# Centring the layer norm on GpSimd ahead of the experts, and no gathered rows in three units before the last stage

## The reference, cut to what matters

```python
def layer_norm(x, g, b):
    mu = jnp.mean(xf, axis=-1, keepdims=True)
    var = jnp.mean(jnp.square(xf - mu), axis=-1, keepdims=True)
    y = (xf - mu) * lax.rsqrt(var + LN_EPS)
    return y * g + b
...
h = layer_norm(ALPHA * h + mix, ln1_g, ln1_b)
ffn = peer_ffn(h, peer_wq, peer_subkeys, peer_u, peer_v)
h = layer_norm(ALPHA * h + ffn, ln2_g, ln2_b)
...
# peer_ffn, for a token: qh = x @ wq; best 16 experts of each head by two sets of sub-keys
act = gelu(einsum('td,thkd->thk', xc, u[expert]))
out = einsum('thk,thkd->td', gate * act, v[expert])
```

## Time and profile before

| | |
|---|---|
| median of 3 runs | 2832.28 us (2826.26 to 2835.13) |
| profiled execution: time | 2836.36 us |
| profiled execution: span from first to last instruction | 2834.5 us |
| mean granted TensorE clock | 0.987 of full speed |
| PE, DVE, ACT, POOL busy | 96%, 68%, 49%, 14% of the span |
| DMA over the span | 236 GB/s |

### The profile page before, as it was taken

One profiled execution on the slowest core, in us unless ns is written; L12 is line 12 of the kernel. 1 busy time (PEld: TensorE's weight loads), 2 busy tenths in 40 slices (PEclk: granted clock), 3 DMA queues, 4 the chain that ended last, 5 costly groups with the idle time before them and its releaser, 6 DMA issues.

```text
span 2834.5 us, 43483 instructions
## 1 busy us (share of the span) xinstructions
PE 2733.1 (96%) x17934; PEld 2557.6 (90%) x17934; DVE 1929.7 (68%) x2867; ACT 1384.3 (49%) x2255; POOL 389.4 (14%) x366
## 2 busy tenths in 40 slices
PE   8999989889999999999999999999999999999996
PEld 8899989889998889979989999998888999988885
DVE  7456578544445455564669657767888888878986
ACT  6356454556555444444453133435555555555554
POOL 0100020211110000005000012221222111113210
PEclk9999999999999999999999999999999999999998
DMA  6444455433335554544544579999999988899993
GB/s 256 163 150 163 149 164 185 140 104 117 102 114 193 193 181 166 189 157 151 179 149 149 202 268 346 359 346 366 377 378 380 345 319 322 324 353 367 371 365 123
DMA packets 109669, 668.28 MB, mean 236 GB/s; under 512 B 25777, under 2 KB 26313, under 8 KB 31553
## 3 DMA queue, kind: packets, MB, share of 16 engines
q1 hardware_dynamic: 83808, 496.08, 48.4%
q0 software_dynamic: 24512, 164.97, 16.0%
q10 hardware_dynamic: 1152, 4.47, 0.4%
HBM read 651.54 MB, written 13.30 MB: 235 GB/s over the span
## 4 chain that ended last, share of the span: by engine, by line
PE 73%; DVE 13%; DMA 7%; ACT 5%; issue 2%; POOL 0%; DVEq 0%; ACTq 0%
PE PS L1178 72%; DMA m<-in_pun,keep 4%; DVE WL L1838 4%; DVE m L1829 3%; ACT WH L2619 2%; DMA m<-in_pv,keep 1%; ACT m L2600 1%; PE PS L1181 1%; DVE m L2084 1%; ACT m L2601 1%; DMA m<-s_kk 1%; DVE m L2081 1%; PE PS L1556 0%; ACT L2600 0%; DVE m L2440 0%
## 5 line engine op out<-in xcount | busy, mean ns | idle before, releaser
L1838 DVE TENSOR_TENSOR WL<-raw,WH 128x1024 fp32r<-128x1024 f32 x708 | 869.0, 1233 | 544.8 <-ACT WH L2619 543.5
L2619 ACT CAST WH<-raw 128x1024 fp32r<-128x1024 f32 x708 | 736.8, 1046 | 393.5 <-PE PS L1178 381.0
L1178 PE MATMUL PS<-m_4096r,WH 128*128 128x256 f32 x4672 | 881.4, 289 | 12.1 <-DVE m L1829 5.2
L1178 PEld LDWEIGHTS PS<-m_4096r,WH 128*128 128x128 f32 x4672 | 734.3, 193 | 17.8 <-DVE m L1829 6.0
L1178 PE MATMUL PS<-m_4096r,WL 128*128 128x256 f32 x2336 | 663.6, 284 | 0.0
L1178 PE MATMUL PS<-WH,m_896r 128*128 128x512 f32 x1536 | 516.6, 390 | 6.5 <-DVE m_896r L2533 3.1
L1178 PEld LDWEIGHTS PS<-m_4096r,WL 128*128 128x128 f32 x2336 | 450.0, 193 | 0.0
L1178 PE MATMUL PS<-WL,m_896r 128*128 128x512 f32 x1024 | 399.1, 390 | 0.0
L1178 PE MATMUL PS<-m_8192r,WH 128*128 128x384 f32 (+1 forms) x1536 | 373.1, 331 | 8.2 <-issue 2.7
L1178 PEld LDWEIGHTS PS<-WH,m_896r 128*128 128x128 f32 x1536 | 289.0, 188 | 68.2 <-DVE m_896r L2533 4.2
L1178 PE MATMUL PS<-m,raw 128*128 128x192 f32 x2048 | 342.0, 326 | 0.0
(11 more groups left out here) (266 smaller groups left out, 2627.8 us busy)
## 6 DMA issues: line engine op xcount, KB each, us to landing
raw<-in_pu SPq DMA_DIRECT2D x112, 1024.0 KB, 7.1
raw<-in_pv SPq DMA_DIRECT2D x96, 1024.0 KB, 8.9
raw<-in_w_qkv SPq DMA_DIRECT2D x48, 1024.0 KB, 4.8
raw<-in_w_o SPq DMA_DIRECT2D x48, 1024.0 KB, 4.8
raw<-in_w SPq DMA_DIRECT2D x40, 1024.0 KB, 4.8
raw<-in_w_z SPq DMA_DIRECT2D x32, 1024.0 KB, 4.8
m<-in_pv SPq DMA_DIRECT2D x32, 1024.0 KB, 8.9
raw<-in_w_kv SPq DMA_DIRECT2D x16, 1024.0 KB, 5.2
```

The source lines that it names most:

```text
L1178: return e.matmul(o, l, x, start=start, stop=stop)
L1838: tt(WL[:, k, :], raw_of(n)[:, h * 1024:h * 1024 + 1024], WH[:, k, :].bitcast(F), ALU.subtract).then_inc(S["lo"], 1)
L2619: e.copy(WH[:, k, :], raw_of(n)[:, h * 1024:h * 1024 + 1024]).then_inc(S["hi"], 1)
```

## The change

The multiplication MR is gone, and so is its buffer. POOL gets a step `h2(c)` that subtracts MU in place from each chunk as soon as MU is there; DVE's `h2(c)` only multiplies by RS, once POOL is done with the chunk. In the walk `prep(2 * WQ)` moves from before the chunks to behind the fourth. POOL's transfer `sub_load` so comes behind its eight subtractions. In U of `peer(1)`, as in U of `peer(0)` already, `pace` is not called in the last three units; the steps of the gathered rows that would have fallen there, and all later ones, come later.

```diff
-                if half or j < 61:
+                if j < 61:
                     self.pace(st, 2 * half)
...
         do("ln1")
-        do("prep", 2 * WQ)
         for c in range(9):
             do("h2", c)
+            if c == 3:
+                do("prep", 2 * WQ)
         do("sub_load")
...
                 recip(RS, RS).then_inc(S["ln1_rs"], 1)
-                v.wait_ge(*at("ln1_rs", 1))
-                v.step(tt(MR, MU, RS, ALU.mult))
...
                     x = k3(X1)[:, 2 * c:2 * c + 2, :]
-                    a = v.step(tt(x, x, bc(RS, 2), ALU.mult))
-                    v.own(a)
-                    tt(x, x, bc(MR, 2), ALU.subtract).then_inc(S["h2_norm"], 1)
+                    v.wait_ge(*at("ln1_rs", 1))
+                    v.wait_ge(*at("h2_mean", c + 1))
+                    tt(x, x, bc(RS, 2), ALU.mult).then_inc(S["h2_norm"], 1)
...
+            def h2(c):
+                if c == 8:
+                    return
+                g_.wait_ge(*at("ln1_mu", 1))
+                x = k3(X1)[:, 2 * c:2 * c + 2, :]
+                tt(x, x, bc(MU, 2), ALU.subtract).then_inc(S["h2_mean"], 1)
```

More of the change, by code:

```diff
@@ L1031, in build @@
         PW = f(88, 2048).rearrange("p (g d) -> p g d", g=8)
-        CM, MU, RS, MR = f(80, 256), f(81, 256), f(82, 256), f(83, 256)
+        CM, MU, RS = f(80, 256), f(81, 256), f(82, 256)
         CM_PART, DEV_PART, SQ_PART, SQ4 = f(88, 512), f(90, 512), f(94, 512), f(84, 1024)
@@ L3232, in gpsimd_program @@
                   "iv_scale": iv_scale, "iv_out": iv_out, "dn_low": dn_low, "dn_y": dn_y, "gate": gate, "x_load": x_load, "bias_load": bias_load, "bias": bias, "ki_out": ki_out,
-                  "pool_loads": pool_loads, "pu_out": pu_out, "sub_load": sub_load, "h_store": h_store,
+                  "pool_loads": pool_loads, "pu_out": pu_out, "h2": h2, "sub_load": sub_load, "h_store": h_store,
                   "c_begin": c_begin, "s_add": s_add, "g_apply": g_apply, "gate_load": gate_load,
```

## The result

The changed kernel took 2833.72 us (median of 20 runs, 2827.98 to 2839.56), the kernel before 2826.64 beside it (20 runs, 2818.73 to 2835.13). The ratio is 1.0023, with an interval of 1.0014 to 1.0031: 6.5 us (4.0 to 8.8) slower. That lies within the 0.3% (8.5 us) that the prediction took as the bound to no change, with the end of the interval just beyond it, and the time lies inside its range. The sum behind it was off by more than 6 us, though: it gave +0.25.

What follows compares the result with a forecast made beforehand. PE holds most of the chain, DVE most of the rest; DVE edits count only where PE stands still. Layer norm +1.25 and V -1.0 give +0.25 on 2836.36, 4.1 above the median: 2832.5 us, range 2825.5 to 2838.

Steps and rivals of the forecast that it cites:

- The sum behind it: Whole kernel: layer norm +1.25 and U-to-V change -1.0 give +0.25 us.
- Layer norm: +1.25 forecast: Layer norm chunks: last low part ends at 1448.1 against 1446.88, 1.25 us later; bounds 1.3 gain to 4 loss.
- DVE keeps its turn while its operations follow without a gap: Layer norm: POOL and DVE alternate by whole operations, and POOL gets in only at gaps in DVE's sequence.
- the schedule: Layer norm: turns of POOL, DVE and ACT played through from DVE's squaring to the last low part at 1448.1.
- the bound without turns: Layer norm: ACT sets the pace, moved cast and low part cost some 1.9; last low part 1445.6, gain 1.3.
- The turn to V: U to V: PE pauses 0.8 us, not 2.75, without slow start; V unit 1 starts 3.7 us sooner.
- V: -1.0 forecast: Early V: DVE stands 7 us for late gather 96, leaving 1.0 of the 3.7 us gained.
- The landing: Early V: gather 96, issued behind HN, LG and LB, lands at 2534.5; due 2527 in unit 3.
- (a): Layer norm: turns don't bite since DVE's operations are short; -1.3 - 1.0, total 2830; chance 0.13.
- (b): V: gathers land in time, -5.8 with the layer norm at +1.25; total 2827.7; chance 0.12.
- (c): V: POOL can't prepare gathers while DVE runs without gaps; +9 to +12, total 2842; chance 0.1.
- (d): New pauses: PE's clock falls and costs more than the slack; +3, total 2835.5; chance 0.1.

Runs made afterwards that it cites:

- pace_alone: Kernel before with only the pacing edit (no pace calls in the last three U units); ratio 1.0010 (0.9998 to 1.0021).
- square_in_four: Kernel before with POOL's two squares of 128 x 2048 each made in four pieces of 128 x 512; ratio 1.0025 (1.0007 to 1.0043).

## Why the prediction was right, and where its steps failed

**The forecast** of no change beyond 0.3% held, and so did its range, but by two errors that offset each other. It stood on a median of three runs, 2832.28, where the 20 runs beside the changed kernel gave 2826.64, 5.6 less; and it made the change 6 us too cheap. That the forecast came within 1.2 us of the measured time is luck.

**Layer norm: +1.25 forecast, +2.8 measured**, inside its bounds (-1.3 to +4). The step that failed is "DVE keeps its turn while its operations follow without a gap". By it multiplication 1 ended 0.6 us after multiplication 0; in fact POOL came between and it was 1.7, and POOL came again ahead of the first low part and of multiplication 2. Counted from DVE's squaring, multiplication 2 ended 2.7 us later than in the schedule and the last low part 1.6 later; POOL, with a turn after each of DVE's operations, was done some 6 us sooner, which made up for part of it. The Trainium skill (SBUF — State Buffer, "SBUF: two separate sides"), which the prediction names there, has the engine that starts first hold the shared pair for the whole instruction. The traces agree with that: beside POOL a multiplication took 1.75 us in place of 0.68. Who comes next is another question, and the rows from which the prediction answered it were one outcome of two, as the square shows. The wait for the moved cast was in the schedule (2.1 us, and 0.5 more for a turn of POOL; measured 2.15), and the bound without turns put the move at some 1.9. But the rivals were set up as turns against no turns, while 2.2 of the 2.8 us hang on one place in ACT's order.

**The turn to V** was right: PE's pause is 0.80 as forecast, the clock stays at 1.00, and the sub-keys' late transfer stayed hidden. The gain is 3.3 us in place of 3.7: 1.95 at the pause, and 1.4 in the first two units (from PE's start to ACT's cast 9.45 us, 10.83 before), where 1.75 were forecast.

**V: -1.0 forecast; +4.1 measured**, +3.3 to +6.6 in the three kernels that have this edit with the loads in their old place. The mechanism was right: gather 96 behind HN, LG and LB, DVE waiting, PE going on 3.81 us after the landing (3.85 forecast). Two terms were mis-sized. The landing was taken at 4.7 us a MB, 24.2 from HN's issue; it took 27.3, exactly the upper of the two figures weighed, so it came 3.1 us later than chosen, and DVE stood for 10.14 us where 7 were forecast. And the prediction let PE go on at full clock, as after the pause of 2.1 us in the earlier trace rows. After 7.64 us it ran at 0.58 for 7 us: 7 x 0.42 = 2.9 us by estimate. The trace of after adds up: -3.3 for the turn, +4.6 for PE's wait of 7.64 in place of 2.11 and 0.95 (of which the forecast had kept the second), and +2.9 for the clock make +4.2.

**The rivals.** (a) is refuted by DVE's 1.75 us, (b) by the wait of 10.14. (c), on the other side, is refuted: the issues took 1.7 to 2.0 us around the late gather, so POOL was not starved. (d) was right in its mechanism, in V above all; its sign in the chunks came too (0.85 of the clock from 1416 to 1439, where before had 0.92 from 1426 to 1447), but what that cost there isn't separated.

## What to carry to other kernels

Before a transfer is made later, list what is issued ahead of it in its own queue: here moving loads that nobody needed yet behind the gathers turned the pacing edit from some 3 us lost (by the medians; the interval leaves room for no loss) into 6 won. When a cut or cast is moved into a loop over two engines, ask whether the pacemaker will stand behind the other engine's last item, since that pause is the price, and the work itself is not. And a rule read from one place in one profile should be looked for in a second execution, above all for which of two engines goes first.

## What the runs showed of the hardware

That one instruction gets its turn after one or after four operations of another engine, in the same code, was not expected: POOL's square took 4.5 us in ten profiles and 7.9 in two. A delay of 3.4 us there goes with 6.6 to 8.2 us more, for PE stands still and then runs at a granted clock of 0.55 to 0.70 over the next 11.5 us (before, pace_alone, square_in_four). Not every DVE operation takes part: the reciprocal beside POOL's third subtraction took its 1.75 us and that subtraction 1.28, while the clamp of 128 x 256 went from 0.29 to 0.82.
